# Recurrence of two RWKV heads at a time: the first two groups' products before the turned values, and the last outputs in two parts

## The reference

```python
def wkv7_scan(r, decay, k, v, kk, a, reverse):
    def step(S, inp):
        r_t, w_t, k_t, v_t, kk_t, a_t = inp
        s_kk = jnp.einsum('bhij,bhj->bhi', S, kk_t)
        S = (S * w_t[:, :, None, :]
             - s_kk[..., None] * (a_t * kk_t)[:, :, None, :]
             + v_t[..., None] * k_t[:, :, None, :])
        return S, jnp.einsum('bhij,bhj->bhi', S, r_t)
    ...
wkv = (wkv7_scan(r4, heads(decay(w0_f, wf_lo, w_up_f)), k_f, v4, kk, heads(a_f), False)
       + wkv7_scan(r4, heads(decay(w0_b, wb_lo, w_up_b)), k_b, v4, kk, heads(a_b), True))
```

## Time and profile before

| | us |
|---|---|
| time, median of 3 runs | 3601.65 (3601.41 to 3604.25) |
| the profiled execution's own time | 3609.76 |
| its span in the profile | 3608.0 |
| PE busy | 3106.3 (86% of the span) |
| PE weight loads busy | 2432.8 (67%) |
| DVE busy | 2077.2 (58%) |
| ACT busy | 1325.4 (37%) |
| POOL busy | 332.4 (9%) |

### The profile page before, as it was taken

The page is one execution under the profiler, slowest core; times in us unless marked ns, Lnnn a source line. Parts: engine busy times, 40 slices in busy tenths (PEclk is TensorE's granted clock), DMA queues, the critical chain, the costliest instruction groups (busy, mean ns, idle before and its releaser), DMA issues. The chain is left out here.

```text
span 3608.0 us, 57788 instructions
## 1 busy us (share of the span) xinstructions
PE 3106.3 (86%) x24483; PEld 2432.8 (67%) x24483; DVE 2077.2 (58%) x2583; ACT 1325.4 (37%) x1763; POOL 332.4 (9%) x231
## 2 busy tenths in 40 slices
PE   6899857699999899777988888867999966999995
PEld 2687655588888788554576665756666645888884
DVE  4443355566666343345567676676211357898985
ACT  2211233321111232346334342443200225777774
POOL 2000011100000000201020111110000000212210
PEclk8899888799999999899998989888999977999997
DMA  4442003211111332202002020101210346999996
GB/s 172 158 158 71 18 18 140 71 47 47 47 52 41 140 117 76 82 6 76 19 3 68 2 69 2 52 2 62 76 41 23 140 187 223 384 400 395 399 393 226
DMA packets 220245, 424.23 MB, mean 118 GB/s; under 512 B 13362, under 2 KB 122884, under 8 KB 219780
## 3 DMA queue, kind: packets, MB, share of 16 engines
q1 hardware_dynamic: 214418, 401.56, 31.0%
q0 software_dynamic: 4608, 16.78, 1.8%
q10 hardware_dynamic: 1013, 2.86, 0.2%
HBM read 387.62 MB, written 33.55 MB: 117 GB/s over the span
## 5 line engine op out<-in xcount | busy, mean ns | idle before, releaser
L213 DVE TENSOR_TENSOR w_exp_low<-w_exp,w_exp_high 128x2048 fp32r<-128x2048 f32 x192 | 438.1, 2291 | 56.4 <-ACT w_exp_high L208 56.2
L208 ACT ACTIVATE w_exp_high<-w_exp 128x2048 fp32r<-128x2048 f32 x192 | 368.0, 1920 | 125.9 <-PE psum L221 125.9
L219 PE MATMUL psum<-ffn_high,w_high 128*128 128x512 f32 x704 | 275.2, 391 | 7.5 <-DVE w_low L213 7.5
L220 PE MATMUL psum<-ffn_low,w_high 128*128 128x512 f32 x704 | 274.9, 390 | 0.0
L221 PE MATMUL psum<-ffn_high,w_low 128*128 128x512 f32 x704 | 274.8, 390 | 0.0
L1513 DVE SCALAR_TENSOR_TENSOR ffn_hidden<-u_padded,param_columns,ffn_hidden 128x1024 f32 (+1 forms) x176 | 226.0, 1284 | 21.1 <-DVE ffn_hidden L1509 1.6
L219 PE MATMUL psum<-w_exp_high,x_turned_high 128*128 128x512 f32 x512 | 203.8, 398 | 7.0 <-DVE w_exp_low L213 7.0
L221 PE MATMUL psum<-w_exp_high,x_turned_low 128*128 128x512 f32 x512 | 201.2, 393 | 0.0
L220 PE MATMUL psum<-w_exp_low,x_turned_high 128*128 128x512 f32 x512 | 201.0, 392 | 0.0
L2471 DVE COPY inverse<-psum 64x512 f32<-64x512 f32 x192 | 121.7, 637 | 75.0 <-PE psum L2306 50.0
L219 PEld LDWEIGHTS psum<-ffn_high,w_high 128*128 128x128 f32 x704 | 132.8, 189 | 35.6 <-DVE w_low L213 7.9
(11 more groups left out here) (518 smaller groups left out, 7587.1 us busy)
## 6 DMA issues: line engine op xcount, KB each, us to landing
w_exp<-in_exp_w_gate SPq DMA_DIRECT2D x32, 2048.0 KB, 12.0
w_exp<-in_exp_w_up SPq DMA_DIRECT2D x32, 2048.0 KB, 11.3
w_exp<-in_exp_w_down SPq DMA_DIRECT2D x32, 2048.0 KB, 13.1
w_raw<-in_w_up SPq DMA_DIRECT2D x44, 512.0 KB, 3.8
ffn_down_ring<-in_w_down SPq DMA_DIRECT2D x44, 512.0 KB, 3.4
ada_weights_late<-in_w_ada SPq DMA_DIRECT2D x16, 1024.0 KB, 6.2
mix_out_ring<-in_w_out SPq DMA_DIRECT2D x32, 512.0 KB, 3.8
mixers_hT<-hidden SPq DMA_DIRECT2D x4, 4096.0 KB, 13.9
```

What stands on the lines that cost most here:

```text
L208: return nc.scalar.activation(out, src, ACT.Copy, scale=scale)
L213: return nc.vector.tensor_tensor(out, src, high.bitcast(F32), ALU.subtract)
L219: nc.tensor.matmul(out, left[0], right[0], start=start, stop=False)
L220: nc.tensor.matmul(out, left[0], right[1], start=False, stop=False)
```

## The change

Three things, all in `stage_rwkv_chunks`, so in each of the four pairs:

1. Opening. PE makes the products of groups 0 and 1 first, one after the other: group 1's go to banks 2 and 3 (`products_bank`), which group 0's mask does not read. The values are turned after them, into banks 4 and 5. ACT copies them as before.
2. The keys of groups 0 and 1 are turned inside the first inverse, at s = 0 and s = 2, and the products of group 2 move from s = 1 to s = 4.
3. The outputs have two parts. `early` holds the 8 products with the states and the 8 with the values; `late` the 8 with `minus_u`. In the middle of the stage they follow each other. At the end, `early(5)` stands after s = 18 of the last inverse, the other parts between the scan's last steps. `late` carries the work of ACT and DVE. The last step's `state` product and its decayed state, which nothing reads, are gone.

```diff
--- before.py
+++ after.py
@@ -2178,24 +2178,34 @@
     def inverse_bank(n, c):
         return 4 + 2 * (n % 2) + c
 
+    def products_bank(n):
+
+        return 2 if n == 1 else 0
+
     def between(n, s):
 
 
         k, at = divmod(s, 5)
         step = (n - 2 + k // 2, k % 2)
         todo = [("right", *step)] if at == 0 else [("solve", *step)] if at == 2 else [("state", *step)] if at == 4 else []
-        todo += {1: [("products", n + 2)], 4: [("outputs", n - 3)], 7: [("products", n + 3)], 11: [("outputs", n - 2)],
-                 14: [("turn", n + 2)], 17: [("turn", n + 3)]}.get(s, [])
+        if n == 0:
+            todo += {0: [("turn", 0)], 2: [("turn", 1)], 4: [("products", 2)]}.get(s, [])
+        else:
+            todo += {1: [("products", n + 2)], 4: [("outputs", n - 3)], 11: [("outputs", n - 2)]}.get(s, [])
+        todo += {7: [("products", n + 3)], 14: [("turn", n + 2)], 17: [("turn", n + 3)]}.get(s, [])
+        if n == TT - 2 and s == 18:
+            todo.append(("early", TT - 3))
         return [t for t in todo if 0 <= t[1] < TT]
 
     def last_steps():
 
-        todo = [("outputs", TT - 3)]
-        for n in (TT - 2, TT - 1):
-            for e in range(2):
-                todo += [(name, n, e) for name in ("right", "solve", "state")]
-            todo.append(("outputs", n))
-        return todo
+
+        n = TT - 2
+        todo = [("right", n, 0), ("late", n - 1), ("solve", n, 0), ("state", n, 0),
+                ("right", n, 1), ("early", n), ("solve", n, 1), ("late", n), ("state", n, 1)]
+        n = TT - 1
+        return todo + [("right", n, 0), ("solve", n, 0), ("state", n, 0),
+                       ("right", n, 1), ("early", n), ("solve", n, 1), ("late", n)]
 
     EVENTS = 2 * L + 1
 
@@ -2223,17 +2233,16 @@
 
         @s.b.tensor
         def _(pe):
-            for t in range(TT):
-                ins = nc.tensor.transpose(ps[:, t // 4, (t % 4) * P:(t % 4 + 1) * P], core.vc[:, t * P:(t + 1) * P],
-                                          core.mask(M_ID))
-            ins.then_inc(vt_mm, 1)
-            pe.wait_ge(vt_out, 1)
-            pe.wait_ge(z_zero, 1)
+            def turn_values():
+                for t in range(TT):
+                    ins = nc.tensor.transpose(ps[:, 4 + t // 4, (t % 4) * P:(t % 4 + 1) * P], core.vc[:, t * P:(t + 1) * P],
+                                              core.mask(M_ID))
+                ins.then_inc(vt_mm, 1)
 
             def products(n):
                 if n >= 2:
                     pe.wait_ge(khT_done, n // 2 * 2)
-                if n % 2:
+                if n % 2 and n > 1:
                     pe.wait_ge(am_done, n)
                     if n >= 6:
                         pe.wait_ge(y_out, n - 5)
@@ -2241,7 +2250,7 @@
                     for part, kind in enumerate((2, 3)):
                         for h, c in ((0, 0), (1, 1), (0, 1), (1, 0)):
                             at = 256 * d + 128 * part
-                            out = ps[rows[c], h, at:at + 128].rearrange("p (k t) -> p k t", k=2)
+                            out = ps[rows[c], products_bank(n) + h, at:at + 128].rearrange("p (k t) -> p k t", k=2)
                             ins = nc.tensor.matmul(out, operand(n, d, c, h, kind), operand(n, d, c, h, slice(0, 2)),
                                                    start=True, stop=True)
                 ins.then_inc(am_mm, 1)
@@ -2340,34 +2349,48 @@
                                                start=(m == 0), stop=(m == 1))
                 ins.then_inc(z_mm, 1)
 
-            def outputs(n):
+            def early(n):
+
                 pe.wait_ge(am_done, min(n + 6, TT))
                 pe.wait_ge(khT_done, min(n + 4 + n % 2, TT))
                 if n:
                     pe.wait_ge(y_out, n)
-                pe.wait_ge(nu_upper, 2 * n + 2)
-                pe.wait_ge(nu_lower, 2 * n + 2)
                 for e in HALVES:
                     for h, c in ((0, 0), (1, 1), (0, 1), (1, 0)):
                         d = c ^ e
                         nc.tensor.matmul(ps[rows[c], h, RN * d:RN * d + RN], operand(n, d, c, h, 1),
-                                         z[rows[h], (2 * n + e) % 4, d], start=True, stop=True)
+                                         z[rows[h], (2 * n + e) % 4, d], start=(e == 0), stop=False,
+                                         skip_group_check=True)
                 for d in DIRS:
                     for h in HEADS:
-                        for m, kind in enumerate((ARK, ARB)):
-                            for c in HALVES:
-                                r, at = rows[c], P + RN * (2 * d + h)
-                                right = vt[r, group(n, d), rows[h]] if m == 0 else nu[r, (2 * n + (c ^ d)) % 4, h]
-                                ins = nc.tensor.matmul(ps[r, c, at:at + RN], am[r, n, h, d, kind], right,
-                                                       start=(m == 0), stop=(m == 1))
+                        for c in HALVES:
+                            r, at = rows[c], P + RN * (2 * d + h)
+                            nc.tensor.matmul(ps[r, c, at:at + RN], am[r, n, h, d, ARK], vt[r, group(n, d), rows[h]],
+                                             start=False, stop=False, skip_group_check=True)
+
+            def late(n):
+                pe.wait_ge(nu_upper, 2 * n + 2)
+                pe.wait_ge(nu_lower, 2 * n + 2)
+                for d in DIRS:
+                    for h in HEADS:
+                        for c in HALVES:
+                            r, at = rows[c], P + RN * (2 * d + h)
+                            ins = nc.tensor.matmul(ps[r, c, at:at + RN], am[r, n, h, d, ARB],
+                                                   nu[r, (2 * n + (c ^ d)) % 4, h],
+                                                   start=False, stop=True, skip_group_check=True)
                 ins.then_inc(y_mm, 1)
 
+            def outputs(n):
+                early(n)
+                late(n)
+
             part = {"right": right_side, "solve": solve, "state": state, "products": products, "turn": turn,
-                    "outputs": outputs}
+                    "outputs": outputs, "early": early, "late": late}
             for n in range(2):
                 products(n)
-            for n in range(2):
-                turn(n)
+            turn_values()
+            pe.wait_ge(vt_out, 1)
+            pe.wait_ge(z_zero, 1)
             for n in range(0, TT, 2):
                 begin(n)
                 begin(n + 1)
@@ -2391,7 +2414,7 @@
         @s.b.scalar
         def _(act):
             act.wait_ge(vt_mm, 1)
-            nc.scalar.activation(vt.ap().rearrange("p t n -> p (t n)"), ps[:, 0:2, :].rearrange("p b n -> p (b n)"),
+            nc.scalar.activation(vt.ap().rearrange("p t n -> p (t n)"), ps[:, 4:6, :].rearrange("p b n -> p (b n)"),
                                  ACT.Copy).then_inc(vt_out, 1)
 
             def turn(n):
@@ -2416,9 +2439,7 @@
                 nc.scalar.activation(rz.ap().rearrange("p h d n -> p h (d n)"), ps[:, 0:2, 0:2 * RN], ACT.Copy
                                      ).then_inc(rz_done, 1)
 
-            part = {"turn": turn, "solve": solve, "outputs": outputs}
-            for n in range(2):
-                turn(n)
+            part = {"turn": turn, "solve": solve, "outputs": outputs, "late": outputs}
             for n in range(0, TT, 2):
                 copy(n, 0)
                 copy(n + 1, 0)
@@ -2461,7 +2482,7 @@
                 dve.wait_ge(am_mm, n + 1)
                 keep = halves[:, H_PRODUCTS:H_PRODUCTS + 8].rearrange("p k t -> p (k t)")
                 for h in HEADS:
-                    ins = nc.vector.tensor_tensor(am[:, n, h].rearrange("p d k t -> p (d k t)"), ps[:, h, :], keep,
+                    ins = nc.vector.tensor_tensor(am[:, n, h].rearrange("p d k t -> p (d k t)"), ps[:, products_bank(n) + h, :], keep,
                                                   ALU.mult)
                 ins.then_inc(am_done, 1)
 
@@ -2479,6 +2500,8 @@
                 dve.wait_ge(rhs_mm, t + 1)
                 extra = tts[:, n % 4, AV].rearrange("p (h e) t -> p h e t", h=2)[:, :, e]
                 nc.vector.tensor_tensor(rhs[:], ps[:, 2:4, 0:RN], extra, ALU.add).then_inc(rhs_done, 1)
+                if t == 2 * TT - 1:
+                    return
                 if t:
                     dve.wait_ge(z_done, t)
                 for d in DIRS:
...
```

More of the change, by code:

```diff
@@ L2517, in _ @@
             dve.wait_ge(z_zero, 1)
-            part = {"products": products, "right": right_side, "solve": solve, "state": state, "outputs": outputs}
+            part = {"products": products, "right": right_side, "solve": solve, "state": state, "outputs": outputs,
+                    "late": outputs}
             for n in range(2):
```

## The result

| | before | changed |
|---|---|---|
| median, same batches (us) | 3602.23 | 3583.78 |
| lowest to highest, 5 runs each | 3601.41 to 3605.53 | 3580.43 to 3587.56 |
| profiled execution's own time | 3609.76 | 3583.78 |

The ratio is 0.9948 (95% interval 0.9936 to 0.9959): 18.5 us less by the medians, 26.0 from one profiled execution to the other. Before's profiled execution lay 7.5 us above its median, so the difference of the profiles is larger than that of the medians.

A forecast was written before the change was run, and what follows sets the result against it. Chains over several engines bound the opening and the end, PE the first inverse. Four pairs x (opening 5.0 + end 1.9) = 27.6 us, taking the median from 3601.65 to 3574.0; range 3562 to 3587.

The forecast's parts named there:

- rival 1: End of each pair: brings nothing, each step's gain handed back at the next; 3582 us, chance 0.17.
- rival 3: Clock stays low into the first inverse and the end's stall returns; 2.75 + 1.0 us a pair, 3587, chance 0.10.
- Opening to the first factor: Each pair's opening: factor(0,1) at 11.05 us instead of 15.90, 4.85 earlier, or 5.7 with begin(1) at the high clock.
- The clock term: Opening and first inverse: 5.45 us a pair if PE's clock rises by begin(1), 2.75 if low until the doublings; 5.0 taken.
- signs of being wrong: begin(1) waiting for something other than DVE, begin(2) for POOL, clock low beyond the first factors, or end not shorter.
- The Trainium skill's rule: Opening: low clock is the default and sustained activity releases it, so inside the new dense stretch; 5.45 us a pair.
- The products of group 2 only change places: zero: First inverse: these products are 32 PE instructions in either order, so moving them costs zero.
- The end: Scan's last steps and outputs: the new order brings 1.9 us a pair, at the low clock with the stall in some pairs.
- The delay by early(5): Before double(7,5) in the last inverse: state(5,1) and its DVE part come 0.65 us later, at the high clock.
- The stall of 1.18 us: Group 6's first step at the end: PE idle without a releaser, counted as gone; if it returns, the end brings 1.0.
- The high-clock end: End of each pair with the high clock all the way: 2.2 + 2 x 0.64 + 2 x 0.43 = 4.4 us.
- rival 4: First inverse: clock misses its rise and stays low, 12.6 us cost, +8.9 a pair, 3637; chance 0.03, other losses included.

The follow-up runs named there:

- e2: The change's end only, with the opening as in the kernel before; 3597.2 us, ratio 0.9985 to the kernel before.
- e4: The changed kernel plus 8 needless transposes behind the turned values and 16 between begin(0) and begin(1); 3578.9 us, ratio 0.9936 to before.
- e3: The changed kernel with the products of group 2 moved from s = 4 to s = 5 of the first inverse; 3587.7 us, ratio 0.9957 to before.
- e9: The changed kernel with early(5) moved from behind s = 18 to behind the state of step 11; 3579.9 us, ratio 0.9937 to before.
- e5: The changed kernel with early(6) and early(7) split, late(6) later and DVE's output additions behind its solve part; 3573.7 us, ratio 0.9905 to before.
- e7: The changed kernel with the edits of e5 and e6 together; 3565.8 us, ratio 0.9887 to before.
- e6: The changed kernel with one of group 0's two factor operations made by POOL, not DVE; 3579.7 us, ratio 0.9929 to before.
- e8: e7 plus 6 needless transposes behind the turned values and 6 between begin(0) and begin(1); 3568.5 us, ratio 0.9896 to before.

## Why the prediction was right in kind and high in size

The forecast was 3574.0, the measured time 3583.8, inside the range, with 18.5 us gained where 27.6 were forecast. It lies outside the forecast's own spread (3567 to 3580), and the number alone stands nearer to rival 1 (3582) and rival 3 (3587); that rival 1 is not what happened is known from e2 and not from the time.

- **Opening to the first factor: right.** 5.35 us gained in the mean of the four pairs (15.90, 15.24, 16.12 and 16.42 us before, 9.74, 11.06, 10.43 and 11.05 after), where 4.85 to 5.7 were worked out, and DVE's factors were what was late next, as said. Pair 1 is below the 10.2 named as the least: the clock was still high for the first 0.6 us of its products, and DVE's mask began at 1.6 us and not at 2.1.
- **The clock term: wrong.** This is the step that failed: "I take 5.0, nearer the first: PE's opening work is now one dense stretch of 5.9 us". The clock did rise in that stretch. I did not follow it further: with the clock up, begin(0) is done at about 7.5 and not at 8.8, DVE still ends at 9.24, and PE waits 1.76 us where I had 0.5. In three pairs the clock fell inside this wait (8.2, 7.5 and 8.5 us after the start), and PE made begin(1), factors, turns and doublings at 1.2 GHz until 15.1, 14.4 and 15.3. So one of the signs of being wrong that the prediction names came true: the clock was low beyond the first factors. e4 shows the cause by removing only the idleness: it gains 5.37 us a pair in the first stretch, about the 5.45 worked out for a high clock. Measured gain of the first stretch 3.77 us a pair, 1.23 below the value taken and inside the ends of 2.75 and 5.45.
- **The Trainium skill's rule** ("TensorE: Matmul & The Clock Gate", section "What's actually happening") gave 5.45 a pair. Its half on the release agrees with the trace (the clock rose 4.0 to 5.1 us after the start, while the values were turned); the same section's default of a low clock without activity is what came true behind the waits, 0.74 in pair 2's second window. I had used one half.
- **"The products of group 2 only change places: zero": right.** e3 moves them one place on, behind the factor pair, and gains nothing; their old place (s = 1) was not tried with the new opening. The turns of the keys beside them were put at 1.05 us for two at the high clock and cost less in this place: from the first factor to double(0,2) it is 6.07 us with them (e4) and 5.78 without (before, pairs 2 to 4), all at a clock of 1.00.
- **The end: right in its steps, and close in size with some luck, 1.80 a pair against 1.9.** The delay by early(5) was put at 0.65; the second stretch grew by 0.79 a pair, and e9 takes 0.55 of it back. The solve behind early(6) came 0.60 later (0.64 forecast), the additions 1.98 behind the solve (1.95). The stall of 1.18 us without a releaser was not at that place in pair 2's end of the changed kernel. The sum counted on such stalls being gone in most pairs and gave no reason for it. They did fall, from 4.3 to 0.6 us over the four ends, and up to 0.9 a pair of the 1.80 is theirs. (The high-clock end was added up to 4.4; its terms give 4.3.)
- **Sum.** Four pairs x (3.77 + 1.80) = 22.3. The profiled executions differ by 3.7 more outside the stages, the medians by 3.8 less; that is within the scatter of single executions here (3068.8 to 3075.8 outside the stages) and stays unexplained.
- Rival 1 (the end brings nothing) is refuted by e2, rival 4 did not happen: even the slowest opening was faster than before by 1.8 us. Rival 3's low clock came in part.

## What to carry to other kernels

When a change makes an engine faster at a place, work out its next wait with the faster times: the gain may turn into idleness, and on PE idleness can cost a second time, in the clock. In a serial chain over several engines, put side work behind the instruction that hands over, not in front of it: the same additions cost 0.9 us in front of the solve's copy (changed kernel) and 0.2 behind it (e5's order, rows of e7). Work that waits can be measured by filling it, but a filled wait shifts everything behind it.

## What the runs showed of the hardware

- PE's clock fell inside a wait of 1.6 to 1.8 us in the opening, behind 5 us of dense products, a wait of 1.1 and begin(0) (pairs 2 to 4 of the changed kernel), and did not in pair 1, with the same instructions and a wait of 1.88. 24 needless transposes in the waits kept it high for the same stretch in all four pairs.
- POOL and DVE slowed each other when both worked on tiles in SBUF: POOL's factors took 2.58 us for 1.79, DVE's addition of the identity 0.72 for 0.42, while DVE's factors, under way beside POOL's, kept their 0.96 (e6, all four pairs).
- PE idles of 0.3 to 1.8 us without a releaser appear at other places in each layout of the program, 0.0 to 3.3 us a pair. They ate part of the first-stretch gain of e4 and e8. The traces point to what they wait for: PE's own instructions. The instruction queue q8 of the page's part 3 brings packets of 16 KB, one for about 258 PE instructions and every 4.3 us (medians inside the stages). All 111 such idles in the four stages of the twelve traces end 1.2 to 1.7 us after a packet's landing, a band of about a tenth of the time between two packets. This is a coincidence in time, though one without an exception; no run moved or removed these packets to try it.
